# Modulation blocks moved between three feed-forward layers, and 512-token borders rebuilt

## The reference

```python
def swiglu_ffn(x, norm_g, w_in, w_out):
    gate, up = jnp.split(rms_norm(x, norm_g) @ w_in, 2, axis=-1)
    return (jax.nn.silu(gate) * up) @ w_out

mx = jnp.split((s_c @ ada_w[i] + ada_b[i])[:, None, :], N_MOD, axis=-1)      # for x
mc = jnp.split((s_cc @ ada_w[i] + ada_b[i])[None, None, :], N_MOD, axis=-1)  # for the context
x = ffn_step(x, norm_g[i, 0], mx[0], mx[1], mx[2], ffn_w_in[i, 0], ffn_w_out[i, 0])
hx = modulate(rms_norm(x, norm_g[i, 1]), mx[3], mx[4])
```

## Time and profile before

| | |
|---|---|
| median of 3 runs | 2832.19 us (2831.08 to 2836.46) |
| the profiled execution's own time | 2833.92 us |
| its span | 2832.3 us |
| PE busy | 2725.0 us, 96% |
| DVE busy | 2049.1 us, 72% |
| ACT busy | 1011.9 us, 36% |
| POOL busy | 139.6 us, 5% |
| granted TensorE clock, mean | 0.981 |

### The profile page before, as it was taken

The page is one execution under the profiler, slowest core; times in us unless marked ns, Lnnn a source line. Parts: engine busy times, 40 slices in busy tenths (PEclk is TensorE's granted clock), DMA queues, the critical chain, the costliest instruction groups (busy, mean ns, idle before and its releaser), DMA issues.

```text
span 2832.3 us, 49047 instructions
## 1 busy us (share of the span) xinstructions
PE 2725.0 (96%) x19250; PEld 2418.7 (85%) x19250; DVE 2049.1 (72%) x3067; ACT 1011.9 (36%) x1167; POOL 139.6 (5%) x204
## 2 busy tenths in 40 slices
PE   6999999999999999999999999998899999999999
PEld 4888878788878888788799899977799989986999
DVE  5877778766777777776676766756767776665677
ACT  4222234222232222333344444553144434443534
POOL 1000011000010000100000000000000010000000
PEclk9999999999999999999999999999999999997999
DMA  8444432533334444322245344521044554443344
GB/s 348 163 174 168 161 150 70 180 136 133 133 124 159 153 180 164 132 90 75 86 176 193 136 178 178 188 86 62 3 169 178 193 142 178 188 168 67 119 185 186
DMA packets 68705, 421.43 MB, mean 149 GB/s; under 512 B 7672, under 2 KB 8824, under 8 KB 26592
## 3 DMA queue, kind: packets, MB, share of 16 engines
q1 hardware_dynamic: 48176, 343.36, 32.8%
q0 software_dynamic: 20432, 76.69, 8.4%
HBM read 418.95 MB, written 1.07 MB: 148 GB/s over the span
## 4 chain that ended last, share of the span: by engine, by line
PE 84%; DVE 9%; issue 3%; ACT 2%; DMA 1%; POOL 1%; SPq 0%; DVEq 0%; ACTq 0%; POOLq 0%
PE ps_o L2230 11%; PE ps_o L2232 10%; PE ps_o L2231 10%; PE ps_g L2230 7%; PE ps_u L2230 7%; PE ps_u L2232 7%; PE ps_u L2231 7%; PE ps_g L2232 7%; PE ps_g L2231 7%; DVE wlo L1261 2%; PE ps_o L2469 1%; DMA scr<-in_AW 1%; DVE tsq L1314 1%; PE ps_g L2253 1%; DVE scr L1475 1%
## 5 line engine op out<-in xcount | busy, mean ns | idle before, releaser
L761 ACT ACTIVATE whi<-wraw 128x2048 fp32r<-128x2048 f32 x314 | 598.8, 1911 | 788.5 <-PE ps_u L2232 371.2
L1261 DVE TENSOR_TENSOR wlo<-wraw,whi 128x2048 fp32r<-128x2048 f32 x314 | 712.3, 2290 | 163.8 <-ACT whi L761 163.7
L2230 PE MATMUL ps_g<-hh,wlo 128*128 128x256 f32 (+1 forms) x1464 | 464.1, 317 | 6.4 <-DVE hl L1327 3.9
L2230 PE MATMUL ps_o<-ah,wlo 128*128 128x256 f32 (+1 forms) x1408 | 454.8, 323 | 15.5 <-DVE x L1367 7.9
L2230 PE MATMUL ps_u<-hh,wlo 128*128 128x256 f32 (+1 forms) x1464 | 462.5, 316 | 0.0
L2232 PE MATMUL ps_g<-hh,whi 128*128 128x256 f32 (+1 forms) x1464 | 462.1, 316 | 0.0
L2231 PE MATMUL ps_g<-hl,whi 128*128 128x256 f32 (+1 forms) x1464 | 462.1, 316 | 0.0
L2232 PE MATMUL ps_u<-hh,whi 128*128 128x256 f32 (+1 forms) x1464 | 462.1, 316 | 0.0
L2231 PE MATMUL ps_u<-hl,whi 128*128 128x256 f32 (+1 forms) x1464 | 461.9, 316 | 0.0
L2231 PE MATMUL ps_o<-al,whi 128*128 128x256 f32 (+1 forms) x1408 | 453.0, 322 | 0.0
L2232 PE MATMUL ps_o<-ah,whi 128*128 128x256 f32 (+1 forms) x1408 | 452.8, 322 | 0.0
(11 more groups left out here) (461 smaller groups left out, 3677.0 us busy)
## 6 DMA issues: line engine op xcount, KB each, us to landing
wraw<-in_W SPq DMA_DIRECT2D x315, 1024.0 KB, 4.8
scr<-in_ADA POOLq DMA_DIRECT2D x126, 512.0 KB, 3.9
scr<-in_AW SPq DMA_DIRECT2D x5, 1024.0 KB, 26.5
big<-in_AW SPq DMA_DIRECT2D x4, 1024.0 KB, 15.4
scr<-bias_rows POOLq DMA_DIRECT2D x8, 384.0 KB, 8.6
x<-in_XT SPq DMA_DIRECT2D x1, 2048.0 KB, 10.3
x<-in_MEMT POOLq DMA_DIRECT2D x2, 1024.0 KB, 6.4
cst<-in_CST POOLq DMA_DIRECT2D x1, 1511.5 KB, 6.7
```

The source lines that it names most:

```text
L761: nc.scalar.activation(whi[:, n % SLOTS, :], wraw[:, n % SLOTS, :], ACT.Copy).then_inc(w_hi, 1)
L1261: tt_(wlo[:, n % SLOTS, :], wraw[:, n % SLOTS, :], whi[:, n % SLOTS, :].bitcast(f32), sub).then_inc(w_lo, 1)
L2230: mm(out, a[1], b[0], start=first, stop=False)
```

## The change

It has six parts.

1. `ADA_PLAN`: feed-forward 0 has 9 blocks ahead (6 before), none in its first round and 5 in each of the other nine (4 in each of ten before); feed-forward 1 has none ahead and 4 a round (8 and 3 before); feed-forward 2 has 2 ahead and 3 a round (2 and 4 before).
2. In a round all blocks now come before the low part of chunk `n0 + 5`, which stood between the second and the third block.
3. The last round of the 512-token feed-forwards is written out apart like that of the others. Its hidden group goes to a buffer of its own (`th`, `tl`, in the upper half of `tsq`), and DVE's work is in another order: first tile, low part of the hidden group, three tiles, a split, four tiles, two tiles of the last `down`, a split, six tiles. With 256 tokens the last split comes one tile earlier than before.
4. Since `tsq` holds that buffer, the squares of tiles 4 to 7 go to `hid` in the norms after feed-forward 0, 1 and 2 (`AFTER_WIDE`).
5. In the same norms POOL adds five squares and PE the rest (`POOLED` 5, before 6), PE's order is now the squares that it adds alone, POOL's sum, and the last square; in three norms (`SUM_HALVES`: after pooling, after feed-forward 1 and after feed-forward 2) PE sums the two halves of the tokens apart, and the first root waits for the first half alone.
6. The norm before the differential attention has no `early` split; the chunk is split behind the norm.

```diff
-ADA_PLAN = ((6, 4), (8, 3), (2, 4))
+ADA_PLAN = ((9, 5, GROUPS - 2), (0, 4, GROUPS - 1), (2, 3, GROUPS - 1))
+SUM_HALVES = (2, 3, 4)
+AFTER_WIDE = (1, 3, 4)
-POOLED = {1: 6, 2: 6, 3: 6, 4: 6, 5: 4, ...
+POOLED = {1: 5, 2: 6, 3: 5, 4: 5, 5: 4, ...
+        last = {NX: (ah2[:, :, NX:NTOK], al2[:, :, NX:NTOK]), NTOK: (th, tl)}
+        def squared_at(k, d, N):
+            return cut(hid, (d - KT // 2) * NTOK, N) if k in AFTER_WIDE and d >= KT // 2 else cut(tsq, d * NTOK, N)
...
-            norm(lambda d: x[:, d, :], NTOK, mod(1, 1), "split", after(FIRST["qkv", 0]), FIRST["qkv", 0], part=3, early=True)
+            norm(lambda d: x[:, d, :], NTOK, mod(1, 1), "split", after(FIRST["qkv", 0]), FIRST["qkv", 0], part=3)
...
+                def blocks(i):
+                    for s in range(per_ada):
+                        ada_block(b0 + s, s, 16 * (fills[s] + 1 - first), i, per_ada)
+                def round_(i, end=False):
+                    done = i * step + DONE[n_down - 1]
...
+                    split_lo(n0 + 5, i, per)
+                    product(i + (g0 + 1), i * step + DONE[n_up], i + (lg + 2))
+                    if not end:
+                        down(n_down, done)
+                        hidden(i + (g0 + 1))
+                        split_lo(n_up + SLOTS, i, per)
+                        split_lo(n_down + SLOTS, i, per)
+                        return
+                    down(n_down, done, range(1))
+                    hidden(i + (g0 + 1), *last[N])
+                    down(n_down, done, range(1, 4))
+                    split_lo(n_up + SLOTS, i, per)
+                    down(n_down, done, range(4, KT))
+                    down(n_last, DONE[n_last - 1], range(2))
+                    split_lo(n_down + SLOTS, i, per)
+                    down(n_last, DONE[n_last - 1], range(2, KT))
...
+                if f == 0:
+                    for b, slot, fill in ahead[6:]:
+                        ada_block(b, slot, 16 * fill)
+                    round_(0)
+                with dve.Fori(first, ffn_loop) as i:
+                    blocks(i)
+                    round_(i)
+                blocks(GROUPS - 2)
+                round_(GROUPS - 2, end=True)
...
-                order = [0] + list(range(POOLED[k], KT))
+                order = [*range(POOLED[k], KT - 1), 0, KT - 1] if k < 7 else [0, *range(POOLED[k], KT)]
...
+                    if k in SUM_HALVES:
+                        for j, half in enumerate(HALVES):
+                            ins = mm(ps_g[:, j, 0:NX], ones, squared_at(k, d, N)[:, half], start=d == order[0], stop=d == order[-1])
+                            if d == order[-1]:
+                                ins.then_inc(nm_sum, 1)
```

More of the change, by code:

```diff
@@ L172, in ada_fills @@
     ahead, per = ada_slots(f)
-    return GROUPS - 1 if slot < per else ahead.count(slot)
+    return ADA_PLAN[f][2] if slot < per else ahead.count(slot)
 STREAM = [("ffn", 0, FFN_TILES), ("pool", 0, [8]), ("ffn", 1, FFN_TILES),
@@ L297, in build @@
         x = sb("x", [128, KT, NTOK])
+        with nc.sbuf_tensor("off_t", [128, KT * NTOK // 2], f32), nc.sbuf_tensor("th", [128, 2, NTOK], f32r) as th, nc.sbuf_tensor("tl", [128, 2, NTOK], f32r) as tl:
+            pass
         tsq = sb("tsq", [128, KT * NTOK])
@@ L479, in ada_ahead, with summed @@
             return [(b0 + q, s, fills[s] + slots[:q + 1].count(s)) for q, s in enumerate(slots)], fills
+        def squared_at(k, d, N):
+            return cut(hid, (d - KT // 2) * NTOK, N) if k in AFTER_WIDE and d >= KT // 2 else cut(tsq, d * NTOK, N)
+        def summed(k, part=1):
+            return k + sum(q < k for q in SUM_HALVES) + 1 + (part if k in SUM_HALVES else 0)
         def pooled(k):
@@ L667, in squares @@
                         pool.wait_ge(nm_acc, pooled(k) + d - 1)
-                    nt(tsq[:, 0:N], tsq[:, 0:N], tsq[:, d * NTOK:d * NTOK + N], add).then_inc(nm_acc, 1)
+                    nt(tsq[:, 0:N], tsq[:, 0:N], squared_at(k, d, N), add).then_inc(nm_acc, 1)
             def ada_begin(f):
-                (b0, _), (n, per) = ADA_RANGE[f], ADA_PLAN[f]
+                (b0, _), (n, per, rounds) = ADA_RANGE[f], ADA_PLAN[f]
                 ahead, _ = ada_ahead(f)
@@ L686, in ada_loads @@
                     ada_load(b, slot)
-                with pool.Fori(0, GROUPS - 2) as i:
+                with pool.Fori(0, rounds - 1) as i:
                     for s in range(per):
@@ L775, in norm @@
                     for d in range(squared, KT):
-                        square(src, N, ready, d)
+                        square(src, N, ready, d, k)
                     if memory is not None or early:
@@ L894, in ffn @@
                     then()
-                with act.Fori(0, ffn_loop(N)) as i:
+                with act.Fori(0, ffn_loop) as i:
                     if f not in LATE:
@@ L1368, in residual, with ffn @@
                 ins.then_inc(o_free, 1)
-            def ffn(f, N, gate, then=None):
+            def ffn(f, N, gate):
                 n0, g0 = FIRST["ffn", f], f * GROUPS
@@ L1416, in ffn @@
                 split_lo(n0 + 3)
-                for b, slot, fill in ahead[5:]:
+                for b, slot, fill in ahead[5:6]:
                     ada_block(b, slot, 16 * fill)
@@ L1773, in _ @@
             ffn(2, NTOK, gate(1, 0))
-            norm(xs_, NTOK, A_mod(1, 1), B_mod(1, 1), "split", part=3, early=True)
+            norm(xs_, NTOK, A_mod(1, 1), B_mod(1, 1), "split", part=3)
             dve.wait_ge(vecs_in, 48)
@@ L2392, in ffn @@
                     down(n_down, i * tiles + TILE0[n_down], i + g0, i)
-                down(n_last, TILE0[n_last], g0 + GROUPS - 1, last=f < 7, a=(last_hi, last_lo) if N == NX else (ah, al))
+                down(n_last, TILE0[n_last], g0 + GROUPS - 1, last=f < 7, a=last[N])
             def ada(n):
```

100 lines of the change are left out of this document (34 added, 66 removed).

## The result

The changed kernel takes 2810.93 us (median of 4 runs, 2807.72 to 2813.78) where the kernel before, run beside it, takes 2834.11 (2831.08 to 2836.46): a ratio of 0.9922, 95% interval 0.9905 to 0.9939, so it is faster, by 0.8%. The forecast was 2812.1, within 2807 to 2820. Two later series of six runs gave 2810.0 and 2809.6 us. The profiled execution took 2813.78 us, its span is 2812.1, against 2832.3 before.

What follows compares the result with a forecast made beforehand. PE was taken as the bound, busy 2725.0 of 2832.3 us, so only its waits and lower clock could pay. Terms summed to 20.04 us, from 2833.92 to 2813.9, less 1.73 for the median: 2812.1 us, range 2807 to 2820.

Steps and rivals of the forecast that it cites:

- 256-token ends: Last split one tile earlier in five 256-token layers: taken as 0, bounds a gain of 1.5 and a loss of 1.
- Blocks inside the rounds: Fifth block in feed-forward 0's rounds leaves DVE -0.05 us before its product, costs nothing; uncovered, at most 20.6 us.
- free lateness: In a 512-token round, DVE's product may come about 3.1 us late without cost to PE.
- First rounds: Fewer blocks ahead of the product remove PE's delays: 0.55 us gained in feed-forward 0, 5.08 in feed-forward 1.
- The last two downs: Own buffer brings last tiles 10.88 us apart: gains 4.40, 4.40 and 2.81 in feed-forward 0, 1, 2, together 11.61.
- The shared interface: DVE split beside POOL's addition at the 512-token ends: 0.5 us lost each by the rule, 1.5 in all; taken as 0.
- The sums: Roots 3.64 and 3.20 us after the last residual starts: gains 0.17 and 0.58 after feed-forward 0 and 1, 1.29 after pooling.
- The border to the attention: Norm before differential attention: reciprocal 2.91 us earlier, 2.15 paid back because the split delays the copy PE waits for.
- smaller gain: Rival, chance 0.17: clock falls at other gaps and half sums cost as much as wholes; gain 12.9 us, time 2819.
- change undone: Rival, chance 0.04: stalls of the 512-token ends move to DVE's residuals; about 5.5 us remain, time 2827.
- larger gain: Rival, chance 0.12: later waits absorb the 2.15 and narrow ends give 1.5; gain 23.7 us, time 2808.5.
- The slower one: Rival, chance 0.04 for slower or nothing: the fifth block's loads come late, blocks 6 us late; above 2838 us.

Runs made afterwards that it cites:

- plan undone: Changed kernel with the old plan of modulation blocks (6 ahead and 4 a round, 8 and 3, 2 and 4), all ahead of the first product: 2818.47 us, ratio 0.9956.
- three more instructions: Changed kernel with three more half-block DVE instructions into unread scratch behind the blocks of every round of feed-forward 0: 2814.81 us (one run).
- One buffer: Changed kernel with the last hidden group of the three 512-token layers back in the one shared buffer: 2820.2 us, ratio 0.9963.
- filled form: The one-buffer kernel with three unread matmuls between the two last downs of the 512-token layers, where PE waited: 2813.21 us, ratio 0.9936.
- halves undone: Changed kernel with each sum of squares as one matmul of 512 columns again, POOL's five squares and the order kept: 2812.03 us (one run).
- eight more DVE instructions: Changed kernel with eight more half-block DVE instructions into unread scratch behind the blocks of every round of feed-forward 0: 2883.74 us (one run).
- early split back: Changed kernel with the last split of feed-forward 2 again ahead of the norm before the differential attention, on ACT and DVE: 2814.16 us (one run).
- sums undone: Changed kernel with POOL adding six squares instead of five, PE summing POOL's result first and no sum halved: 2819.88 us (one run).
- reordered kernel: Changed kernel with DVE's queue at the attention border reordered: lambda products ahead of the norm, first query copies ahead of the late split: 2808.03 us, again 2806.06 us.

## Why the prediction was right, and where it was not

| term | predicted | measured | from |
|---|---|---|---|
| first round of feed-forward 0 | 0.55 | 0.55 (0.31 in one of three executions) | first round |
| first round of feed-forward 1 | 5.08 | 5.06 | RP-H1 |
| end and sums of feed-forward 0 | 4.40 + 0.17 | 4.72 | H0-R0 |
| sums after pooling | 1.29 | 1.29 | R0-RP |
| end and sums of feed-forward 1 | 4.40 + 0.58 | 5.17 | H1-R1 |
| end of feed-forward 2 and border | 2.81 + 2.91 - 2.15 | 5.11 - 2.44 | R1-R2, R2-R3 |
| sum | 20.04 | 19.46 | |
| 256-token ends, behind R3 | 0 | some 1.0 | last hidden part to root |

The spans of the two traced executions differ by 20.2 us; the remaining 0.7 lies outside: R3 to the end is 1.1 shorter, the way to the first round 0.3 longer. Executions with the same code behind R3 differ by up to 10.8 us there.

That the whole time came out 1.2 us from the forecast is in part luck. The clock that the forecast left out at one border (1.15 us) and the ends that it had at nothing (some 1.0) nearly cancel, and the difference between the medians of the two kernels was 23.2, 21.5 and 24.0 us in the three series. What is right is the sum over the stretch, term by term.

- **Blocks inside the rounds: right in effect, one number wrong.** Five blocks a round cost nothing: the plan undone has the same H0-R0. The forecast left DVE -0.05 us before its product; the trace leaves 1.30. The step that failed is 2.24 - 2.29: before, the split stood among the blocks and waited there 1.45 us for ACT's high part; behind the blocks it finds it ready, and DVE's waiting ahead of the product is longer by that. So the free lateness of 3.1 us wasn't needed. It exists, though: with three more instructions the product of a steady round began 8.68 us ahead of the hidden part instead of 10.78, 2.1 us later, at no cost.
- **First rounds: right.** The delay in feed-forward 1 was the queue of blocks, both wait and clock, as its return with the plan shows. The gain of 5.08 was what the kernel before had lost there; in the plan undone the same wait cost 6.3, so the size of its clock part isn't fixed.
- **The last two downs: right.** The last tile comes 4.40 us earlier behind H0 in feed-forward 0, 4.41 behind H1 in feed-forward 1 (806.48 - 501.91 against 822.18 - 513.20) and 2.79 behind R1 in feed-forward 2, predicted 4.40, 4.40 and 2.81. DVE catches up at tile 6 of the last down, where the count without POOL had said 5. One buffer and its filled form show the two parts, 2.7 of wait and 1.6 of clock a layer.
- **The shared interface: right to cost it at nothing for DVE at these ends, but it isn't nothing for POOL.** DVE's split beside POOL's addition took 2.28 us, not 2.80 as at the earlier trace rows, so DVE wasn't late by it. POOL's addition took 2.60, twice its 1.3 alone. The Trainium skill (GPSIMD Engine Reference, Key points) says that the two contend for shared interfaces when the VectorE instruction has two SBUF inputs; the trace agrees with it. Which of the two pays went by which started first, at the places read: the split started 0.84 us ahead here, at the earlier trace rows the addition 0.08 ahead, and there both were longer. The change survives the longer addition since POOL adds one square fewer; with six it is late by 2.1 us.
- **The sums: right within 0.2.** Roots 3.49 and 3.02 us after the last residual starts, predicted 3.64 and 3.20. (The new order of PE's sums holds after pooling too, as the prediction has it.) A half is worth 0.41 us (the halves undone), predicted 0.43.
- **The border to the attention: a term missing.** Reciprocal at 1177.94 - 1174.34 = 3.60 us, predicted 3.77; PE's restart 23.6 us behind it instead of 21.6, so 2.05 paid back, predicted 2.15. But the forecast counted the wait and not the clock behind it. From PE's restart to R3 it was 1411.00 - 1221.85 = 189.15 us before and 1391.87 - 1201.57 = 190.30 after: 1.15 lost, behind a restart with a clock of 0.91 where it had been 1.00. So this border gave 3.08 - 2.05 - 1.15 = -0.1 us where 2.91 - 2.15 = 0.76 was forecast. Whether the early split by itself is worth taking off stays open, by the run that puts it back; DVE's queue in another order is worth 3.5 us there. The forecast had asked of each wait that it removed what clock stood behind it, and did not ask it of the wait that it added.
- **256-token ends: a term put at nothing that gave some 1.0 us.** Whole stretches behind R3 are too spread to show it, the distance from the last hidden part to the root is not. At two of the five ends it was 16.27 and 16.30 us, and it is 15.80 to 15.86 in all thirteen executions of kernels with the change. At the first of these two DVE's split of 2.80 us held back the residual for which PE waited. It now stands one tile earlier and starts ahead of POOL's addition. Of the kernel before:

```profile
1807.52 0.39 PE L2230 MATMUL ps_o<-ah,wlo 128*128 128x256 f32 x1 [0.77 <-DVE x L1367]
```

and of the changed kernel:

```profile
1786.45 2.28 DVE L1273 TENSOR_TENSOR wlo<-wraw,whi 128x2048 fp32r<-128x2048 f32 x1
1787.06 2.25 POOL L680 TENSOR_TENSOR tsq<-tsq 128x256 f32<-128x256 f32 x1 [189.80 <-ACT tsq L777]
...
1789.12 0.39 PE L2244 MATMUL ps_o<-ah,wlo 128*128 128x256 f32 x1 [0.25 <-DVE x L1379]
```

The split is back to 2.28 us, and PE waits 0.5 us less; the other of the two ends has the same rows. No run takes this part back alone, so the cause is read from the rows only. The first end changed by less than 0.1 us, the last is 0.1 to 0.2 shorter (15.03 us from its last hidden part to the end of the span, now 14.84 to 14.93), and the remaining one lies between 17.9 and 19.3 us whatever the kernel.

Of the rivals, the smaller gain falls with its two conditions (no low clock at the ends, halves at half price), and so does the change undone: no wait of PE on residuals above 0.5 us. Of the larger gain one half came in part: the narrow ends gave 1.0 of its 1.5 us, but later waits absorbed nothing of the 2.15, and clock came on top. The slower one asked for blocks 6 us late: its mechanism is real, at eight more DVE instructions a round it costs 74 us, but at three more it isn't there yet.

## What to carry to other kernels

Ask of every wait of TensorE, removed or added, what clock stands behind it: at waits of 2.5 to 3.2 us the clock's part was mostly a third to a half of the cost, at times nothing, and where the gap was filled with matmuls that nobody reads, it was given back. Before a queue's head is lightened for one consumer, look at what else stands in it: a split behind the norm made the reciprocal 3.1 us earlier and held the copies on which TensorE waited; moving short copies ahead of the long split, and small scalar steps into idle time, gave both. Measure a change of parts by distances between marks inside the trace: over most stretches they repeat to 0.1 us, where whole times spread over 8 to 15. And where such a distance agrees with a theory, look at the stretches inside it: with the early split back the sum agreed with a theory, while a low clock in one place and a full one in another, which it didn't have, stood against each other.

## What the runs showed of the hardware

- **The same gap doesn't cost the same clock.** A gap of 3.2 us was followed by 1.9 us of loss in one kernel and 3.1 in another; the stall of 2.5 us in feed-forward 2 by none in the kernel before and by 1.5 with one buffer. At the border a wait of 2.55 to 2.57 us stood ahead of a granted clock of 0.91 to 0.93 over the next 20 us in eight executions, and ahead of 1.00 in two (the sums undone, eight more on DVE). What decides it stays open. The two executions with R2-R3 at 215.9 us are like the others at the border; they differ 160 to 180 us behind the restart, with a granted clock of 0.82 and 0.83 against 0.87 to 0.90 where R2-R3 is 214.4 to 214.6 and the clock fell at the border.
- **A split of DVE and an addition of POOL that overlap.** Where the split started first, it kept its 2.28 us, and the addition ended 1.2 us after it (397.98 + 2.60 against 397.14 + 2.28, 512 columns, 1.3 alone) or 0.6 us (1787.06 + 2.25 against 1786.45 + 2.28, 256 columns, 0.75 alone). Where the addition started 0.08 us ahead, both were longer, 2.80 for the split and 2.60 for the addition.
- **A stretch of slower matmuls at full granted clock.** In one execution of the reordered kernel the 256-token layer behind the attention ran 169 matmuls in each window of 20 us, where another kernel's execution has 174. One window of each, the reordered kernel's first run and then the changed kernel's second (of its three traced executions):

```profile
1428.00:1448.00 20.00, 20.00 (x169) 1.00 0.56 204
```

```profile
1430.50:1450.50 20.00, 20.00 (x174) 1.00 0.58 224
```

Over nine such windows 3% is 5 us, and the distance of the roots around it was longer by as much (199.5 us against 193.0, of which some 1.8 is a granted clock of 0.91 in its first window). That is up to 6.5 of the 10.8 us by which executions differ behind R3; other distances there vary by 5 us and more as well (the last between two roots from 127.1 to 132.4), and what they consist of wasn't read. The cause is open.
